# Adding the gate halves of feature-major FFN chunks on VectorE instead of by accumulating DMA

## What is computed

```
def swiglu(x, w_in, w_out):
    gate, up = jnp.split(x @ w_in, 2, axis=-1)
    return (jax.nn.silu(gate) * up) @ w_out
```

## Time and profile before

| | us |
|---|---|
| median of 3 runs | 965.91 (965.4 to 967.02) |
| the profiled execution | 964.49 |
| its span, first to last instruction | 962.8 |
| TensorE busy | 952.3 |
| VectorE busy | 849.0 |
| ScalarE busy | 620.4 |
| GpSimd busy | 108.7 |
| accumulating DMAs for gates | 64 of 128 KB, median 4.9 to landing |

### The profile page before, as it was taken

How to read it: one execution, slowest core, us unless ns; L and a number is a source line. 1 busy time by engine, 2 the same in 40 slices (tenths; PEclk the granted TensorE clock), 3 DMA queues, 4 the chain that set the end, 5 groups by cost and what they waited for, 6 DMA issues and landing times.

```text
span 962.8 us, 13790 instructions
## 1 busy us (share of the span) xinstructions
PE 952.3 (99%) x4904; PEld 806.8 (84%) x4904; DVE 849.0 (88%) x1174; ACT 620.4 (64%) x727; POOL 108.7 (11%) x146
## 2 busy tenths in 40 slices
PE   9999999999999999999999999999999999999996
PEld 7888888888888888888888888888888888888885
DVE  5999998996898999889889989899898997999886
ACT  6776667436646667675576666549998546667660
POOL 0211111100210111110011101100100100111110
PEclk9999999999999999999999999999999999999999
DMA  9778877753656786876587777935243656786761
GB/s 306 240 228 234 280 235 223 232 178 129 223 180 205 217 244 193 236 227 206 173 237 235 239 231 232 271 124 184 89 131 115 235 192 190 215 242 194 237 162 55
DMA packets 140912, 197.31 MB, mean 205 GB/s; under 512 B 7280, under 2 KB 114336, under 8 KB 140720
## 3 DMA queue, kind: packets, MB, share of 16 engines
q1 hardware_dynamic: 126032, 173.56, 55.3%
q0 software_dynamic: 14256, 22.38, 11.1%
q10 hardware_dynamic: 560, 0.52, 0.2%
HBM read 182.79 MB, written 1.06 MB: 191 GB/s over the span
## 4 chain that ended last, share of the span: by engine, by line
PE 91%; DVE 5%; ACT 2%; issue 1%; DMA 1%; POOL 0%; DVEq 0%; SPq 0%; ACTq 0%
PE psum L2012 23%; PE psum L2026 15%; PE psum L2019 12%; PE psum L1821 12%; PE psum L1830 12%; PE psum L1825 12%; DVE w_lo L995 1%; PE psum L2402 1%; ACT w_hi L503 1%; PE psum L1814 1%; PE psum L2388 1%; DVE w_lo L1031 1%; DMA raw<-in_ffn_w_out 1%; DVE w_lo L1001 1%; PE psum L1996 1%
## 5 line engine op out<-in xcount | busy, mean ns | idle before, releaser
L995 DVE TENSOR_TENSOR w_lo<-raw,w_hi 128x2048 fp32r<-128x2048 f32 x125 | 285.1, 2284 | 20.9 <-ACT w_hi L503 20.8
L2012 PE MATMUL psum<-xT,w_hi 128*128 128x512 f32 x1024 | 254.2, 390 | 0.5
L503 ACT CAST w_hi<-raw 128x2048 fp32r<-128x2048 f32 x125 | 238.3, 1914 | 24.5 <-DMA raw<-in_ffn_w_in 15.0
L2012 PEld LDWEIGHTS psum<-xT,w_hi 128*128 128x128 f32 x1024 | 191.3, 188 | 44.8 <-ACT ffn_tok L573 3.2
L2019 PEld LDWEIGHTS psum<-xT,w_lo 128*128 128x128 f32 x1024 | 139.7, 190 | 10.0
L2019 PE MATMUL psum<-xT,w_lo 128*128 128x256 f32 x1024 | 142.8, 282 | 0.0
L1821 PE MATMUL psum<-w_hi,xT 128*128 128x512 f32 x447 | 128.7, 399 | 0.8 <-DVE arena L1538 0.4
L1830 PE MATMUL psum<-w_hi,xT 128*128 128x512 f32 x447 | 124.8, 390 | 0.2 <-DVE xT L1099 0.2
L1825 PE MATMUL psum<-w_lo,xT 128*128 128x512 f32 x447 | 124.7, 390 | 0.0
L1717 POOL DMA_DIRECT2D ffn_tok<-ffn_tok x64 | 55.0, 859 | 484.7 <-ACT ffn_tok L573 484.7
L1830 PEld LDWEIGHTS psum<-w_hi,xT 128*128 128x128 f32 x447 | 83.9, 188 | 18.3 <-DVE xT L1099 0.5
(11 more groups left out here) (220 smaller groups left out, 1165.3 us busy)
## 6 DMA issues: line engine op xcount, KB each, us to landing
raw<-in_ffn_w_in SPq DMA_DIRECT2D x170, 512.0 KB, 5.2
raw<-in_ffn_w_out SPq DMA_DIRECT2D x88, 512.0 KB, 4.4
raw<-in_c_w_in SPq DMA_DIRECT2D x32, 512.0 KB, 4.7
ffn_tok<-ffn_tok POOLq DMA_DIRECT2D x64, 128.0 KB, 4.9
raw<-in_ab_w_in SPq DMA_DIRECT2D x16, 512.0 KB, 4.9
x_tok<-arena POOLq DMA_DIRECT2D x16, 256.0 KB, 7.3
raw<-in_ab_w_o SPq DMA_DIRECT2D x8, 512.0 KB, 4.2
raw<-in_c_w_o SPq DMA_DIRECT2D x8, 512.0 KB, 4.0
```

The source lines that it names most:

```text
L503: nc.scalar.copy(w_hi[:, slot_of[n]], raw[:, n % RAW]).then_inc(hi_ready, 1)
L995: nc.vector.tensor_tensor(w_lo[:, slot_of[n]], raw[:, n % RAW], w_hi[:, slot_of[n]].bitcast(F32), ALU.subtract).then_inc(lo_ready, 1)
L2012: nc.tensor.matmul(G[0], w_hi[:, slot_of[n + kh], at:at + P], xT_both[:, 4 * kh + k].rearrange("p a s -> p (a s)"), start=kh == k == 0, st ...
```

## The change

Chunks 2 and 3 keep the accumulating DMAs. In chunks 4 to 9 of each FFN call GpSimd issues none; VectorE adds both gate blocks' halves in one call, behind split_lo of the second unit and ahead of split_plain_lo, and the silu waits for that. GpSimd's other loads stay where they were written.

```diff
 FIRST_FM = 2
+N_BY_DMA = 2
 N_FM = NC - 1 - FIRST_FM
@@
-        gate_added = [sem(f"gate_added{j}") for j in range(2)]
+        gate_added, gate_summed = [sem(f"gate_added{j}") for j in range(2)], sem("gate_summed")
@@
             def gates_silu(name, c):
 
-                for j in range(2):
-                    act.wait_ge(gate_added[j], 16 * (N_FM * SILUS[name] + c - FIRST_FM + 1))
+                f, k = SILUS[name], c - FIRST_FM
+                if k < N_BY_DMA:
+                    for j in range(2):
+                        act.wait_ge(gate_added[j], 16 * (N_BY_DMA * f + k + 1))
+                else:
+                    act.wait_ge(gate_summed, (N_FM - N_BY_DMA) * f + k - N_BY_DMA + 1)
                 nc.scalar.activation(GATES[:, :, 0:SEQ], GATES[:, :, 0:SEQ], ACT.Silu).then_inc(gate_silu, 1)
@@
+            def gate_sum(name, c):
+
+                dve.wait_ge(up_copied, 4 * (N_FM * SILUS[name] + c - FIRST_FM) + 2)
+                nc.vector.tensor_tensor(GATES[:, :, 0:SEQ], GATES[:, :, 0:SEQ], GATES[:, :, SEQ:], ALU.add
+                                        ).then_inc(gate_summed, 1)
@@
                     split_lo(n + 2)
+                    if c >= FIRST_FM + N_BY_DMA:
+                        gate_sum(name, c)
                     if c < last:
                         split_plain_lo(n + 3)
@@
             def add_gates(name, chunks):
                 for c in chunks:
-                    for j in range(2):
+                    for j in range(2 if c < FIRST_FM + N_BY_DMA else 0):
                         pool.wait_ge(up_copied, 4 * (N_FM * SILUS[name] + c - FIRST_FM) + j + 1)
                         pool.dma_start(GATES[:, j, 0:SEQ], GATES[:, j, SEQ:], accum_op=ALU.add).then_inc(gate_added[j], 16)
```

## The result

The changed kernel takes 973.44 us (median of 6 runs, 973.18 to 974.07) against 966.70 for the kernel before (6 runs, 965.40 to 967.02): ratio 1.0073, 95% interval 1.0063 to 1.0084. It is slower by 6.7 us. The forecast was +1.2, with the range ending at 970.0.

A forecast was written before the change was run, and what follows sets the result against it. TensorE was taken as the bound, busy 952.3 of 962.8 us. VectorE's lateness in F0 cost 1.2, all else nothing: 964.49 + 1.2 = 965.7, or 967.1 on the median; range 965.0 to 970.0.

The forecast's parts named there:

- the burst and the lateness overlap: F0: the early 2 MB of loads and late VectorE share stalls up to about 1 us; nothing added.
- the lower bound: F0's chunk 4: poolw down at 66.7, band meets only the unit's last 0.9 us; landing 0.9 later, price nothing.
- The upper bound: F0's chunk 4: band beside a w_in unit stretched a half unit to 7.7 us against 4.8, 2.9 later.
- rival 1: Cast at 67.59, F0's chunk 4: even sharing lands weights 4.3 us later; +3.2, 969.1; chance 0.28.
- The rule weighed: DMA engines alternate between queue rows by whole packets, so GpSimd's loads take half from the weights; spoke against the change.
- no gain from the 48 DMAs: Steady beat: no wait ends with the removed accumulating DMAs, so their going gives nothing there; ceiling anywhere 3.2 us.
- the steady beat: Steady chunks: the new 0.69 us VectorE add fits in the 1.05 us gap ahead of L1001; costs nothing.
- VectorE's lateness in F0: F0's chunks 5 to 7, no gap for the adds: stalls 0.61, 0.42 and 0 to 0.38; 1.2 us taken.
- the refund: F0: while TensorE stands, VectorE works on, and what it catches up of its 1.27 us comes off the stalls.
- F2's loads at nothing: F2: gam_few store about a chunk earlier, both gam loads (1 MB) behind it, meeting weights; taken as nothing.

The follow-up runs named there:

- e6: The changed kernel with the whole 2 MB of GpSimd's loads issued behind the second copy of F0's chunk 7; ratio 1.0033.
- e1: The changed kernel with GpSimd still waiting for the gate copies of chunks 4 to 9, so its loads go out when they did before; ratio 1.0004.
- e9: The changed kernel with F0's gates by DMA through chunk 6 and GpSimd's loads behind chunks 4, 5 and 6 as before; ratio 1.0010.
- e10: The changed kernel with GpSimd's waits kept and one more VectorE add of the same size behind each gate add; ratio 1.0025.
- e8: The changed kernel with poolw, band and gain rows spread behind the second copies of F0's chunks 7, 8 and 9; ratio 1.0011.
- e4: The changed kernel with GpSimd's waits kept in F0 alone, F2's store and gam loads staying early; ratio 1.0011.
- e5: The changed kernel with 1.5 MB early (poolw, band, gain row); the bias row waits for chunk 6's second copy; ratio 1.0040.
- e3: The changed kernel with 1 MB early (poolw, band); both gain loads wait for chunk 6's second copy; ratio 1.0014.
- e7: The changed kernel with F0's gates by DMA through chunk 6 and GpSimd's loads spread behind chunks 7, 8 and 9; ratio 1.0022.

## Why the prediction was wrong

- **Failed: "up to about 1 us the burst and the lateness overlap rather than add, and I add nothing".** It rested on the lower bound, that poolw's 6.9 us would keep band and the gain rows away from the w_in unit, so that it would land 0.9 later. It landed 7.1 us later (75.11 - 67.56, less 0.42), TensorE stopped for 5.6 us and ran at the low clock behind that. The issues of the changed kernel show how; the columns are those of the earlier trace rows, and the w_in row is for both halves of that unit (11.7 and 13.2 us, from 61.31 and 61.88):

```profile
raw<-in_ffn_w_in SPq DMA_DIRECT2D x2, 512.0 KB, 12.5
arena<-shape_constants POOLq DMA_DIRECT2D x1, 768.0 KB, 8.3
...
ln_gb<-in_ln_gain POOLq DMA_DIRECT2D x1, 512.0 KB, 9.5
ln_gb<-in_ln_bias POOLq DMA_DIRECT2D x1, 512.0 KB, 10.9
arena<-in_pool_w POOLq DMA_DIRECT2D x1, 256.0 KB, 6.5
```

  From their issue in the timeline above, poolw was down at 66.7, band at 69.3, gain at 71.0 and bias at 73.0, the unit's first half at 73.0 too and its second only at 75.1. Poolw did land when I said; that held nothing back. A part of its 6.9 us is its place behind a gate DMA: in e6, with none ahead of it, it took 5.0.
- **The upper bound was cut short.** For the price from above I took the one case in the trace, 2.9 us late for 0.75 MB, and rival 1 capped the rest by even sharing: 4.3. The rows spoke against even sharing already: 2.9 us is not "nearly all" of the 2.2 us that band takes at the full rate, as I wrote, but more than all of it. The plain scaling, 2.9 x 2 / 0.75 = 7.7 us, was in the same two rows and came out near the 7.1 measured, in part by luck: 2.9 compares a second half with the median of all transfers, and the second half of the unit at 67.59 took 6.1 us without any band beside it. e6, with 2 MB and 4.7 us, doesn't fit it. Still, where a burst is nearly three times the one seen, its cost has to be scaled, and the range must hold the scaled value: landing 75.3, a stop of 6.8 us, above 972.
- **The rule weighed.** The Trainium skill, DMA: Bandwidth & Descriptors, section on queues, rings and completion order, has each engine take turns between queue rows, a packet at a time. I read that as equal bytes. The changed kernel's trace counts what each queue moved from 64 to 72 us, q0 being GpSimd's and q1 that of SyncE's weights (packets, MB, share of 16 engines):

```profile
q0 software_dynamic: 639, 2.20, 76.7%
q1 hardware_dynamic: 645, 0.67, 25.8%
```

  The turns are equal, 639 and 645 packets, and so this trace agrees with the rule; the bytes are more than three to one. By these counts a packet of the weights carried 1 KB and one of queue 0 3.4 KB on average: a row of the w_in unit is cut into pieces of 256 columns, and band and the gain rows go in pieces of 6 and 4 KB. e6 shows the same from 130 to 134 us, 306 packets each for 1.24 and 0.31 MB. At 353 GB/s the weights would have moved 2.8 MB in those 8 us and moved 0.67; what is missing is worth 6.1 us, my estimate of the burst's part in the 7.1. No run changed the length of the pieces.
- **Missing: the clock.** I had no term for it. In the trace before, TensorE's longest single wait is 1.1 us, and the clock is full from the first chunk until the last 4 us of the span. The low clock took 3.0 of the 8.4 us.
- **Rival 1 had the right place and the right instruction** (the cast at 67.59) and weights held up by the burst, but by even sharing, with a chance of 0.28 and a price of 3.2 us, against 8.4 in F0's profile.
- **Right: no gain from the 48 DMAs.** e1, e9: none that can be measured. F1 and F3 were as long as before to 0.03 us and 0.3 us.
- **Right: the steady beat.** The add fits in L1001's gap, and e10 shows that a second one would.
- **Right in kind, about twice too large: VectorE's lateness in F0.** The forecast had 0.61 for chunk 5, 0.42 for chunk 6 and up to 0.38 for chunk 7. TensorE lost 0.3 (e6, e8) to 0.5 (e1, e4) in chunk 5, 0.3 in chunk 6 (e4, e6, e8) and nothing in chunk 7 (e6, e8): 0.6 to 0.8 against 1.2. Of the 1.24 by which e1's F0 is longer, 0.77 stands behind the wait for raw, which e9 shows with no gate added on VectorE up to there. In the changed kernel the lateness didn't show at all: TensorE's stop let VectorE catch up, as the refund said.
- **F2's loads at nothing:** 0 to 0.5 us in the profiles.
- **Not foreseen: executions differ at the seams** by up to 2 us, more than the term I argued about. The execution of the earlier trace rows was one that lost nothing there, and lay under its median for that, at least in part. That would also explain why the profiles show 8.4 us in F0 alone and the medians only 6.7 us in all.

## What to carry to other kernels

When instructions leave a queue, list what they were holding back: here 6 waits on GpSimd paced four loads, and without them 2 MB of parameters took most of the bandwidth from the weights that TensorE needed next. Keep the wait when you drop the work behind it. Price a burst by the packets and bytes that each queue moves in a stretch where both are busy, not by an even share of bytes, and add that a long stop of TensorE is paid again in clock.

## What the runs showed of the hardware that I had not expected

- While GpSimd's and SyncE's queues both had work, each moved about as many packets (639 and 645; in e6 306 and 306), and the bytes went by the size of the packets: 2.20 against 0.67 MB. GpSimd's last load, issued at 62.07, was down at 73.0; half a MB of weights issued at 61.88 was down at 75.1. The engines together moved 320 to 400 GB/s.
- After a stop of 5.6 us the granted clock was 0.50 for about 6.8 us; after one of 3.1 us (e5), for about 3.4 us; after 2.0 us (e3) and 1.8 us (e6), not at all.
- One kernel's undisturbed executions differ by 4 us and more (e9, 965.22 to 969.52), and beside the longest waits for the first weights behind F0 (1.0 us in e1, 4.8 in e7 and e9) up to 2 us of that can be seen.
